# Gathering the first two expert tiles with products: rows stationary, one-hot columns streaming, results feature-major

## The reference, cut to what matters

```python
group_logits = xf @ w_group                    # 4 groups
g_idx = argmax(group_logits)                   # the best group
top_logit, top_j = lax.top_k(sel, 2)           # its best two of 8 experts
combine = sum(one_hot(e_idx, 32) * weights)    # g_w * softmax(top_logit)
a, b = x @ w_gate[e], x @ w_up[e]              # 1024 -> 256 each
y = (silu(a) * b * combine) @ w_down[e]        # 256 -> 1024
x = x + g2 * y
```

## Time and profile before

| | us |
|---|---|
| runs of the kernel before, median of 3 | 794.14 |
| lowest and highest of them | 793.38, 794.16 |
| the profiled execution, its own time | 792.12 |
| its span | 790.3 |
| PE busy | 661.8 |
| DVE busy | 296.2 |
| ACT busy | 137.7 |
| POOL busy | 123.5 |
| HBM traffic over the span, GB/s | 383 |

### The profile page before, as it was taken

How to read it: one execution, slowest core, us unless ns; L and a number is a source line. 1 busy time by engine, 2 the same in 40 slices (tenths; PEclk the granted TensorE clock), 3 DMA queues, 4 the chain that set the end, 5 groups by cost and what they waited for, 6 DMA issues and landing times.

```text
span 790.3 us, 12671 instructions
## 1 busy us (share of the span) xinstructions
PE 661.8 (84%) x4657; PEld 351.4 (44%) x4657; DVE 296.2 (37%) x725; ACT 137.7 (17%) x328; POOL 123.5 (16%) x196
## 2 busy tenths in 40 slices
PE   3899999999998899999645667997899997564586
PEld 3343343446795565555312323645655553221232
DVE  2205418674217434444311132557344444112123
ACT  3111134552136200000000000655000000000000
POOL 1000000001000223443211001010233343111110
PEclk9999999999998899999966689999899999677689
DMA  9999769959088689999999999998499999999996
GB/s 334 425 430 430 308 236 367 391 237 402 20 357 344 199 325 418 417 420 417 420 422 420 423 423 360 425 421 357 163 417 418 420 418 417 425 419 424 420 413 250
DMA packets 39737, 291.43 MB, mean 369 GB/s; under 512 B 7546, under 2 KB 8978, under 8 KB 20608
## 3 DMA queue, kind: packets, MB, share of 16 engines
q1 hardware_dynamic: 30112, 272.46, 83.6%
q0 software_dynamic: 7760, 13.13, 4.8%
q10 hardware_dynamic: 1808, 5.06, 1.6%
HBM read 285.20 MB, written 17.56 MB: 383 GB/s over the span
## 4 chain that ended last, share of the span: by engine, by line
PE 60%; DMA 29%; DVE 4%; SPq 2%; issue 2%; ACT 2%; DVEq 0%; ACTq 0%
PE bank L1719 17%; DMA adaw<-in_moe_w_in 9%; PE bank L1423 8%; DMA ring<-in_moe_w_in 8%; PE bank L1756 7%; DMA adas<-in_moe_w_in 7%; PE bank L1348 4%; PE bank L1522 4%; DMA ring<-in_ada_w 4%; PE bank L1678 2%; DMA rows<-qkv 2%; PE bank L1530 2%; PE bank L1461 2%; PE bank L1482 2%; PE bank L1585 1%
## 5 line engine op out<-in xcount | busy, mean ns | idle before, releaser
L1719 PE MATMUL bank<-ring,qkv 128*32 128x256 f32 (+1 forms) x1344 | 141.9, 442 | 48.2 <-DMA ring<-in_moe_w_in 32.4
L1719 PEld LDWEIGHTS bank<-ring,qkv 128*32 128x32 f32 (+1 forms) x1344 | 79.1, 139 | 95.2 <-issue 66.4
L1193 DVE COPY qkv<-bank 128x512 f32<-128x512 f32 x46 | 31.8, 692 | 207.3 <-PE bank L1678 193.5
L600 POOL DMA_INDIRECT results<-adaw,scur x46 | 47.4, 1029 | 266.5 <-DVE adaw L1216 243.5
L866 ACT ACTIVATE qkv<-bank 128x128 f32<-128x128 f32 x48 | 13.3, 278 | 419.6 <-PE bank L1719 401.5
L1423 PE MATMUL bank<-ring,hT 128*128 128x512 f32 x144 | 65.5, 610 | 1.3 <-DVE hT L946 1.3
L1756 PE MATMUL bank<-ring,qkv 128*32 128x512 f32 (+1 forms) x368 | 65.7, 601 | 0.0
L1719 PE MATMUL bank<-seventh,qkv 128*64 128x256 f32 (+1 forms) x224 | 36.0, 490 | 15.7 <-DMA ring<-in_moe_w_in 15.7
L590 POOL DMA_INDIRECT adaw<-rows,gcur x40 | 41.7, 1042 | 32.9 <-POOL gcur L587 22.5
L1719 PE MATMUL bank<-adaw,qkv 128*64 128x256 f32 (+1 forms) x256 | 36.5, 449 | 10.1 <-DMA adas<-in_moe_w_in 10.1
L1423 PEld LDWEIGHTS bank<-ring,hT 128*128 128x128 f32 x144 | 27.3, 194 | 38.1 <-issue 36.9
(11 more groups left out here) (264 smaller groups left out, 840.8 us busy)
## 6 DMA issues: line engine op xcount, KB each, us to landing
ring<-in_moe_w_in SPq DMA_DIRECT2D x37, 2048.0 KB
ring<-in_moe_w_out SPq DMA_DIRECT2D x44, 1024.0 KB
ring<-in_ada_w SPq DMA_DIRECT2D x14, 2048.0 KB, 14.7
adaw<-in_ada_w SPq DMA_DIRECT2D x10, 2048.0 KB, 15.1
adaw<-in_moe_w_in SPq DMA_DIRECT2D x8, 2048.0 KB
seventh<-in_moe_w_in SPq DMA_DIRECT2D x8, 1792.0 KB, 26.3
xT<-in_moe_w_in SPq DMA_DIRECT2D x8, 1536.0 KB
hT<-in_moe_w_out SPq DMA_DIRECT2D x10, 1024.0 KB
```

What stands on the lines that cost most here:

```text
L600: pool.indirect_dma_start(res, bass.IndirectOffsetOnAxis(ap=scur[:, p, :], axis=0), yout[:, p], None, bounds_check=res_limit, oob_is_err=F ...
L1193: V.tensor_copy(xgT[:, p], bank[2][:, :]).then_inc(xgT_ready, 1)
L1719: last = T.matmul(bank[p][64 * a + m * h:64 * a + m * (h + 1), 0:2 * P], xk[:, k % 4, k // 4, m * h:m * (h + 1)], gate_up_of(b, k)[:, :, a ...
```

## The change

The first two tiles, not the first alone, are formed by products, and the product is turned around: 128 columns (features) of `rows_out` are stationary and the one-hot tile `dg` moves, 128 columns of it, 64 places of tile 0 and 64 of tile 1. The result is feature-major, so no transposes follow. It goes to banks 1 and 4, and ACT copies it from there to `xgT` of both tiles. `rows_T` of tiles 0 and 1, the copy to `xg` and DVE's copy of tile 1 are gone; POOL's first gathers are those of tiles 2 and 3. One product of the identity follows the stream and counts `xg_mm` up by two.

The six row blocks go to banks 4, 5, 0, 6, 4, 5, all ahead of the counts, and their copies write contiguously; the host lays the gate/up weights out for that order of features. The filler has 8 products instead of 10. The band load waits for tile 2's gather.

```diff
+        ROW_BANKS = (4, 5, 0, 6, 4, 5)
+        FIRST = 2
+        FIRST_BANKS = (1, 4)
...
-                    sp.wait_ge(s_xg[1], 16)
+                    sp.wait_ge(s_xg[FIRST], 16)
...
-                for b in range(1, NBUF):
+                for b in range(FIRST, NBUF):
...
-                    A.activation(rows_out[:, t, :].rearrange("p (k q) -> p q k", k=KD)[:, 64 * q:64 * q + 64, :],
-                                 bank[4 + n % 2][:, :].rearrange("p (q k) -> p q k", k=KD), ACT.Copy)\
+                    A.activation(rows_out[:, t, 512 * q:512 * q + 512], bank[ROW_BANKS[n]][:, :], ACT.Copy)\
...
-                act.wait_ge(tab_mm, l * 3 + 1)
-                act.wait_ge(xg_clear, l * 2 + 2)
-                A.activation(xg[:, 0], bank[1][:, :], ACT.Copy).then_inc(texp, 1)
-                act.wait_ge(xg_mm, l * NS + 1)
                 act.wait_ge(s_rowsout, l * 48 + 48)
-                A.activation(xgT[:, 0], bank[2][:, :], ACT.Copy).then_inc(xgT_ready, 1)
+                for a in range(2):
+                    act.wait_ge(tab_mm, l * 4 + FIRST)
+                    A.activation(xgT.rearrange("p b (i a c) -> p i a b c", i=4, a=2)[:, :, a],
+                                 bank[FIRST_BANKS[a]][:, :].rearrange("p (i b c) -> p i b c", i=4, b=2), ACT.Copy)\
+                        .then_inc(xgT_ready, 1)
...
-                order(V.tensor_scalar(first, tile_at, 0.0, None, ALU.is_equal))
+                order(V.tensor_tensor(first, tile_at.unsqueeze(1).to_broadcast(of_first),
+                                      C("tiles")[:, 0:FIRST].unsqueeze(2).to_broadcast(of_first), ALU.is_equal))
...
-                rows_T(1, 1, old=False)
                 hidden(0, 0, old=False)
...
-                    if n >= 2:
-                        pe.wait_ge(hb_copied, l * 6 + n - 1)
+                    if n >= 4:
+                        pe.wait_ge(hb_copied, l * 6 + n - 3)
...
-                for n in range(5):
+                for n in range(6):
                     rows_by_token(n)
...
+                pe.wait_ge(hb_copied, l * 6 + 4)
...
-                rows_by_token(5)
-                busy(10)
+                busy(8)
...
-                for t in range(TT):
-                    for a in range(2):
-                        last = T.matmul(bank[1][64 * a:64 * a + 64, :], dg[:, t, 64 * a:64 * a + 64],
-                                        rows_out[:, t, a * 512:(a + 1) * 512], start=t == 0, stop=t == TT - 1,
-                                        skip_group_check=True)
-                last.then_inc(tab_mm, 1)
+                for a in range(2):
+                    for i in range(4):
+                        for t in range(TT):
+                            last = T.matmul(bank[FIRST_BANKS[a]][:, i * P:(i + 1) * P],
+                                            rows_out[:, t, (4 * a + i) * P:(4 * a + i + 1) * P], dg[:, t],
+                                            start=t == 0, stop=t == TT - 1)
+                    last.then_inc(tab_mm, 1)
+                T.matmul(bank[0][:, 0:P], ident, ident, start=True, stop=True).then_inc(xg_mm, 2)
...
-                rows_T(0, 0, old=False)
                 token_table()
+                pe.wait_ge(xgT_ready, l * NS + 2)
                 gate_up(0, 0, old=False)
                 result_table()
-                rows_T(1, 1)
...
-    v["moe_w_in"] = np.stack([w.reshape(depth, NE, P, KD, FE) for w in (gate, up)], 4).reshape(depth, NE, P, KD * 2 * FE)
+    v["moe_w_in"] = np.stack([w.reshape(depth, NE, KD, P, FE).transpose(0, 1, 3, 2, 4) for w in (gate, up)], 4).reshape(depth, NE, P, KD * 2 * FE)
```

More of the change, by code:

```diff
@@ L1135, in router @@
                 order(V.tensor_tensor(place_at, slot, tile_at, ALU.subtract))
-                first, first_place = rt[:, 12:18], rt[:, 18:21]
-                order(V.tensor_scalar(first, tile_at, 0.0, None, ALU.is_equal))
[L1138 to L1141, removed]
+                first = rt[:, 12:24].rearrange("p (n i) -> p n i", n=FIRST)
+                first_place = rt[:, 24:30].rearrange("p (t n) -> p t n", t=TT)
+                of_first = [P, FIRST, 6]
+                order(V.tensor_tensor(first, tile_at.unsqueeze(1).to_broadcast(of_first),
+                                      C("tiles")[:, 0:FIRST].unsqueeze(2).to_broadcast(of_first), ALU.is_equal))
+                order(V.scalar_tensor_tensor(first, place_at.unsqueeze(1).to_broadcast(of_first), 1.0, first, ALU.add, ALU.mult))
+                order(V.scalar_tensor_tensor(first_place, first[:, :, 0:3].rearrange("p n t -> p t n"), -1.0,
+                                             first[:, :, 3:6].rearrange("p n t -> p t n"), ALU.add, ALU.add))
+                to_place = [P, TT, FIRST, TC]
+                V.tensor_tensor(dg[:, :, :].rearrange("p t (n c) -> p t n c", n=FIRST),
+                                C("place")[:, 0:TC].unsqueeze(1).unsqueeze(1).to_broadcast(to_place),
+                                first_place.unsqueeze(3).to_broadcast(to_place), ALU.is_equal).then_inc(slots_ready, 1)
                 by_tile, by_place = [P, 6, NT], [P, 6, P]
@@ L1155, in router @@
                 order(V.tensor_reduce(gbest, ge.rearrange("p (t g) -> p t g", t=TT), AX.X, ALU.add))
-                dve.wait_ge(texp, l * 2 + 1)
+                dve.wait_ge(texp, l + 1)
                 order(V.tensor_scalar(m1, far, 1.0, None, ALU.add))
@@ L1160, in router @@
                 order(V.tensor_tensor(wts[:, 1, :], wts[:, 0, :], far, ALU.mult))
-                dve.wait_ge(tab_mm, l * 3 + 2)
+                dve.wait_ge(tab_mm, l * 4 + 3)
                 V.tensor_scalar(gidx[:, :], bank[3][:, 0:NT], 2.0, C("half"), ALU.mult, ALU.add).then_inc(idx_ready, 1)
@@ L1175, in router @@
                 V.tensor_copy(extra_e[0:1, :], rt[0:1, 80:81 + EXTRA]).then_inc(x_down[l], 1)
-                dve.wait_ge(tab_mm, l * 3 + 3)
+                dve.wait_ge(tab_mm, l * 4 + 4)
                 V.tensor_scalar(sidx[:, :], bank[6][:, 0:NT], 2.0, C("half"), ALU.mult, ALU.add).then_inc(idx_ready, 1)
@@ L1594, in rows_by_token @@
                     t, q = n // 2, n % 2
-                    if n >= 2:
-                        pe.wait_ge(hb_copied, l * 6 + n - 1)
+                    if n >= 4:
+                        pe.wait_ge(hb_copied, l * 6 + n - 3)
                     for k in range(4):
-                        last = T.transpose(bank[4 + n % 2][:, k * P:(k + 1) * P], hT[:, 4 * q + k, t * P:(t + 1) * P], ident)
+                        last = T.transpose(bank[ROW_BANKS[n]][:, k * P:(k + 1) * P], hT[:, 4 * q + k, t * P:(t + 1) * P], ident)
                     last.then_inc(hb_mm, 1)
-                for n in range(5):
+                for n in range(6):
                     rows_by_token(n)
@@ L1667, in rows_T @@
                 def rows_T(s, q, old=True):
[L1668 to L1671, removed]
+                    pe.wait_ge(s_xg[q], 16 * (users(l, q, NBUF) + s // NBUF + 1 - (l + 1 if q < FIRST else 0)))
                     if old:
```

## The result

The changed kernel took 789.62 us, median of 16 runs (786.20 to 792.61), the kernel before 793.67, median of 16 beside them (791.21 to 796.78): ratio 0.995, 95% interval 0.9934 to 0.9967, or 4.05 us less. The forecast was 3.35 us less.

What follows compares the result with a forecast made beforehand. Expert-weight DMA was taken as the limit, its start set by when `gate_up(1)` frees a weight slot. Layer 0's 1.5 and layer 1's 1.85 us sum to 3.35, from median 794.14 to 790.8 us; range 788.3 to 794.8.

Steps and rivals of the forecast that it cites:

- Row blocks and store: Ahead of the router's counts: last store some 6 us earlier in layer 0, no longer ending last; PE's chain late next.
- The stream: PE's 48 records between `dg` and token table: 5.36 us from 259.5 in layer 0; `gate_up(0)` starts 0.1 us later.
- `gate_up(0)` at full clock: Tile 0's gate/up products: unpaused 128-column stream keeps 2.4 GHz, so 3.62 us instead of 5.07 in layer 0.
- Tile 1: Its transposes and DVE's copy ahead of `hidden(0)` go, bringing `gate_up(1)` forward: -0.69 us a layer.
- The gate rows: PE's products ahead of `gate_up(1)`: 3.69 us, mostly at half clock, with no gain counted outside rival B.
- main case: Case A, the sum as worked: 790.8 us, within 789.6 to 792.0; chance 0.45.
- rival B: No half-clock stretch in these stages; gate rows about 1.9 us, layer 1 gives 4.05: 788.6 us; chance 0.13.
- DMA gap of layer 0: DMA idle 2.20 us between router and second expert tile; closes as `gate_up(1)` ends 2.0 us earlier.
- cap of 1.5 us: Layer 0: once the DMA gap closes, only 1.5 us of the 2.0 count.
- E: New stream at 1.2 GHz from end to end: 795.6 us in one layer, some 800 in both; chance 0.12.
- D: `gate_up(0)` falls to half clock as before in both layers: 793.4 us, no change told; chance 0.10.
- C: Clock lost in layer 1 only, after PE idles before `dg`: +1.7 us there, 792.5 us; chance 0.20.

Runs made afterwards that it cites:

- e1: Kernel before with the row-block part alone (six blocks in four banks ahead of the counts, contiguous copies, new feature order): ratio 0.9967.
- e9: Kernel before with the row blocks alone, measured a second time: ratio 0.9969.
- e7: Changed kernel with the row blocks alternating between banks 4 and 5 again, the sixth behind the router's counts: ratio 0.9994.
- e3: Kernel before with five filler identity products more a layer in PE's pauses, three during ACT's copy and two behind the token table: ratio 0.9982.
- a0: The changed kernel again, unaltered, as control: ratio 0.9978.
- e5: Changed kernel with PE making the gate rows before it turns tile 0's hidden rows: ratio 0.9905.

## Why the prediction was right, point by point

The time, the sign and the size were right: 3.35 us forecast, 4.05 measured. The sum hides two terms that were mis-sized, the start of `gate_up(0)` and the gate rows, and one cause that was wrong, that of the clock in `gate_up(0)`. The first two are of opposite sign and nearly cancel (+1.2 and -0.9 us a layer), so that the total came so near is in part luck.

*Row blocks and store: right on the store, wrong on what it is worth.* The last store was issued at 5.1 to 5.2 us behind the router and never released ACT's copy in the changed kernel. But I wrote that what is late next is PE's own chain, and gave the blocks no gain of their own. e1 and e9 give them 2.5 us, e7 nothing to the rest without them. By stages their gain is the clock of `gate_up(0)`, below, and no earlier start: in e1 and e9 it starts 20.0 us behind the router in the mean, before 19.4. How the blocks bring that about, and what the rest of the 2.5 us is, stays open.

*The stream: mis-sized.* I took 5.36 us at full clock from 259.5. It measured 6.60 and 6.59 in the first profile and 5.5 to 5.7 in the other four passes: 0.115 to 0.117 us a record at full clock instead of 0.1116, and in the first profile the clock came back only some 2.2 us after it had begun. My working let layer 0 be at full clock from the first record. Hence `gate_up(0)` starts 20.2 to 21.6 us behind the router, mean 20.62, against 18.9 to 20.2 before, mean 19.42: 1.2 us later, not 0.1 to 0.6.

The working also took 3.4 us for the filler's 16 records at half clock, where twice 0.1116 makes 3.57; they took 3.5 to 3.8. For layer 1 it had the clock still at 0.50 when the stream was to start, which the earlier trace rows does not show; a window of the kernel before does:

```profile
543.70:545.90 2.20, 2.20 (x11) 1.90 (x12) 2.03 (x8) 1.36 (x3) 0.00 (x0) 0.50 1.02 408
```

*`gate_up(0)` at full clock: right in value, wrong in cause.* 3.67 us in six of six passes against a mean of 4.87 before: -1.2 us, as forecast. But the step "PE streams 128-column products without a pause" is not what does it: e1, e9 and e3 keep the old product, the old transposes and the pause or part of it, and have 3.67 in six of six. Their common ground is that PE has less idle time between `dg` and `gate_up(0)`: 1.25 us in the mean of the four passes before, 0.7 in each of e1 and e9, 0.5 in the mean of e3, none in the changed kernel. That this is the cause is argued and not shown; in e3 one pass still idled 1.05 us and kept the clock, and before one with 0.96 kept it. The Trainium skill ("TensorE: Matmul & The Clock Gate", Part 4) says that transposes do not count as activity for the clock in the way that products do. In e1, e9 and e3 the transposes stayed in front of `gate_up(0)`, and it ran at full clock all the same (3.67 us), so taking them out was not needed here.

*Tile 1: right.* 0.6 us a layer by the traces, for a forecast of 0.69.

*The gate rows: missed.* In the main case I let them and `gate_up(1)` take what they took. Before, they together take 7.65 to 7.70 us in four of four passes; after, a mean of 6.78. That is 0.9 us a layer, half of rival B, which I gave 0.13: in three of the six passes they took 6.05 us, in the other three 7.26 to 7.64. It makes good most of what the stream lost.

*DMA gap of layer 0: half right.* In the first profile `gate_up(1)` came only 0.6 us sooner, counted from the router, and the gap stayed. Windows of after and of a0, around the wait for refill 8:

```profile
280.30:281.40 1.10, 1.10 (x10) 0.57 (x6) 0.00 (x0) 0.28 (x1) 0.00 (x0) 1.00 0.03 11
```

```profile
277.40:278.50 1.10, 1.10 (x10) 0.62 (x6) 0.00 (x0) 0.28 (x1) 0.00 (x0) 1.00 0.90 358
```

In a0 it is closed, as forecast. The band load sets refill 7 as I had it: the refill follows it by 1.34 us in both, and goes out 26.62 us behind the router after and 25.22 in a0, against 25.49 before. But the cap of 1.5 us that I set on layer 0 does not stand: from the router of layer 0 to that of layer 1 it is 286.37 and 285.76 us before, 282.77 in a0 and 282.25 in e5, some 3 us less or more, though in the first profile (287.53) nothing was gained.

*Rivals.* E (the stream at half clock from end to end) did not come about; it ran at half clock for at most about a third of its time. D did not either. C's loss of clock was seen in neither layer's stream beyond those 2.2 us.

*Taken together.* Counted by stages the sum is +1.2 (later start) -1.2 (`gate_up(0)`) -0.6 (tile 1) -0.9 (gate rows) = -1.5 a layer, 3.0 us in all. The interval of the measurement, 2.6 to 5.2 us, holds it.

## What to carry to other kernels

Before a reordering is moved into TensorE, count its records and not their moving columns: here 48 records took the same time with 64 and with 128 moving columns, so the second tile's columns were free. Measure the parts of a change one by one: the row blocks, which I had priced at nothing, gave about 2.5 us alone where the whole change gave 4.05, and without them the rest gave nothing that could be measured. Look behind the change for where the engine idles next: moving the gate rows, work that was due anyway, into PE's pause behind the result table took the ratio from 0.9978 to 0.9905, measured side by side, about as much as the change itself or more; filler in the same pause gave nothing that could be measured. And where one kernel's stage varies by 3 us with the place of its half-clock stretches, compare several profiles or stages, never one pair of ends.

## What the runs showed of the hardware

Float32 records with 128 stationary columns took 0.117 us each whether 64 or 128 columns moved (5.64 against 5.62 us for 48). The same program on the same chip spread from 785.23 to 794.54 us; in the 16 runs of the changed kernel the two with the lowest granted clock of the execution (0.915) took 791.67 and 792.61 us and the one with the highest (0.925) 786.20. The clock fell to 1.2 GHz (granted clock 0.50) after stretches in which PE paused for ACT or DVE, though not after each: behind the same pause at the result table it fell in three of six passes of the changed kernel and held in three. Five filler products in such pauses (10 records, some 1.1 us at 0.1116 us each, an estimate) went with the full clock behind them in two of two passes where the kernel without them had it in one of four.
